# A decoder layer on one core: the last two feed-forward blocks and the per-layer-embedding stage laid out anew

## The reference, cut to what matters

```
hn = rms_norm(h, norm_ffn_w)
gate_pre, val = split(hn @ ffn_w_up)              # 2 x 2816 columns
gate = causal_dwconv(gate_pre, conv_w, conv_b)    # width 3 over the tokens
h = h + (silu(gate) * val) @ ffn_w_down           # 2816 -> 1024
h = h + sigmoid(h @ ple_gate_w) * (p @ ple_w)     # 1024 x 1024, 256 x 1024
return rms_norm(h, final_norm_w)
```

## Time and profile before

| what | us |
|---|---|
| median of three runs (lowest, highest) | 1751.04 (1747.47, 1751.82) |
| the profiled execution, its own time | 1752.36 |
| the profiled execution, its span | 1750.6 |
| PE busy in the span | 1652.4 (94%) |
| DVE busy | 1049.7 (60%) |
| ACT busy | 627.9 (36%) |

### The profile page before, as it was taken

The page is one execution under the profiler, slowest core; times in us unless marked ns, Lnnn a source line. Parts: engine busy times, 40 slices in busy tenths (PEclk is TensorE's granted clock), DMA queues, the critical chain, the costliest instruction groups (busy, mean ns, idle before and its releaser), DMA issues.

```text
span 1750.6 us, 22237 instructions
## 1 busy us (share of the span) xinstructions
PE 1652.4 (94%) x8157; PEld 1334.8 (76%) x8157; DVE 1049.7 (60%) x2090; ACT 627.9 (36%) x1169; POOL 84.9 (5%) x126
## 2 busy tenths in 40 slices
PE   8899999997889999999999999999999999997894
PEld 6688888897656766678888888888888888876673
DVE  6734556555799999854455556556555565546233
ACT  5214344345677777632321221122122122113121
POOL 0101211220000000000000000000000000000002
PEclk9999999998699999999999999999999999998997
DMA  5433232235000000230221121121111112102002
GB/s 192 135 101 115 89 122 87 74 121 160 22 16 13 13 13 1 84 146 1 72 73 37 36 72 36 36 70 38 36 56 52 36 43 64 48 0 96 1 37 84
DMA packets 48874, 110.57 MB, mean 63 GB/s; under 512 B 8864, under 2 KB 17056, under 8 KB 48800
## 3 DMA queue, kind: packets, MB, share of 16 engines
q1 hardware_dynamic: 41376, 85.47, 14.9%
q0 software_dynamic: 7424, 24.12, 4.1%
HBM read 89.65 MB, written 19.92 MB: 63 GB/s over the span
## 4 chain that ended last, share of the span: by engine, by line
PE 81%; DVE 9%; ACT 3%; issue 2%; DMA 1%; POOLq 0%; POOL 0%; DVEq 0%; ACTq 0%
PE ps L1434 27%; PE ps L1088 13%; PE ps L1090 13%; PE ps L1089 13%; PE ps L1234 3%; PE ps L1350 3%; PE ps L1307 2%; PE ps L1313 1%; PE ps L1421 1%; PE ps L1093 1%; PE ps L1352 1%; PE ps L1257 1%; PE ps L1353 1%; DMA out<-ost 1%; DVE mx L1799 1%
## 5 line engine op out<-in xcount | busy, mean ns | idle before, releaser
L1939 DVE TENSOR_TENSOR h<-h,ps 128x512 f32<-128x512 f32 x352 | 236.4, 687 | 158.3 <-PE ps L1090 157.0
L1434 PE MATMUL ps<-htl,wuh 128*128 128x512 f32 x672 | 209.8, 393 | 0.0
L1434 PE MATMUL ps<-hth,wuh 128*128 128x512 f32 x672 | 209.7, 393 | 0.0
L1434 PE MATMUL ps<-hth,wul 128*128 128x512 f32 x672 | 209.7, 393 | 0.0
L1088 PE MATMUL ps<-wh,xth 128*128 128x512 f32 (+1 forms) x448 | 186.7, 417 | 14.6 <-DVE wl L1531 13.0
L1090 PE MATMUL ps<-wh,xtl 128*128 128x512 f32 (+1 forms) x448 | 170.9, 382 | 0.0
L1089 PE MATMUL ps<-wl,xth 128*128 128x512 f32 (+1 forms) x448 | 170.4, 380 | 0.0
L1030 ACT ACTIVATE ffh<-ffa 128x1024 fp32r<-128x1024 f32 x22 | 23.4, 1062 | 381.7 <-DVE ffa L1956 381.7
L1434 PEld LDWEIGHTS ps<-hth,wuh 128*128 128x128 f32 x672 | 126.3, 188 | 29.4
L1434 PEld LDWEIGHTS ps<-hth,wul 128*128 128x128 f32 x672 | 126.2, 188 | 29.2
L1434 PEld LDWEIGHTS ps<-htl,wuh 128*128 128x128 f32 x672 | 126.3, 188 | 28.9
(11 more groups left out here) (269 smaller groups left out, 3206.4 us busy)
## 6 DMA issues: line engine op xcount, KB each, us to landing
wuraw<-in_w_up SPq DMA_DIRECT2D x44, 512.0 KB, 5.5
wraw<-in_w_in SPq DMA_DIRECT2D x48, 256.0 KB, 3.3
proj_d<-stage POOLq DMA_DIRECT2D x48, 256.0 KB, 2.4
wdraw<-in_w_down SPq DMA_DIRECT2D x22, 512.0 KB, 3.5
rin<-proj_d POOLq DMA_DIRECT2D x32, 256.0 KB, 4.0
xraw<-in_xt SPq DMA_DIRECT2D x16, 256.0 KB, 6.1
owraw<-in_w_out SPq DMA_DIRECT2D x8, 512.0 KB, 5.8
h<-in_x SPq DMA_DIRECT2D x1, 4096.0 KB, 16.0
```

The lines of the kernel that those rows point to most:

```text
L1434: mm = nc.tensor.matmul(ps[:, 2 * part + half, :], w_, x_[:, k, half * 512:(half + 1) * 512], start=(k == 0 and i == 0), stop=(k == NK - 1 ...
L1939: nc.vector.tensor_tensor(hh, hh, ps[:, 4 + o_ % 4, :], ALU.add).then_inc(dn_add, 1)
```

## The change

The whole end from block 21 on is written anew.

- **The last two blocks' down products.** `down_part(o_, u)` adds block 20 (u = 0) and block 21 (u = 1) in the same bank, so a unit has six matmuls and one `down_add`. Block 21's value part has nothing woven in. Units 0 to 3 have their first halves right behind it, then come the embedding products of units 0 and 1 into banks 0 and 1 (`part_product`), then the second halves. Block 20 leaves PE's loop and stands in straight code.
- **Weights.** `ple_w` is loaded behind the last feed-forward loads, `pt` after block 20's value part, and both are split by ACT and DVE ahead of their work for block 21 (`part_high`, `part_low`). The gate weights have a place of their own where `hth`/`htl` lay, eight pieces of 128x2x512; their loads are issued together when block 21's value part is done. DVE splits them between the adds by the table `WITH_ADD`.
- **The units** go tile by tile (`t, half = divmod(n, 2)`). Transposes go two tiles ahead, into a ring of three tile buffers (`gth`, `gtl`); the first two stand among the down units (`TURN_ADD`).
- **The norm.** ACT squares each half into a buffer of its own (`sqj`) as soon as it is added; nothing waits for a store there. Each tile is normed while the next one is computed, and the last tile is normed and stored in two halves.

```diff
+        g = Region(nc, START)
+        gwh, gwl, gwraw = [], [], []
+        for i in range(NK):
+            gwh.append(g.put(f"gwh{i}", [P, 2, CH], F32R))
+            gwraw.append(nc.alloc_sbuf_tensor_at(f"gwraw{i}", [P, 2, CH], F32, offset=g.at))
+            gwl.append(g.put(f"gwl{i}", [P, 2, CH], F32R))
+        assert g.at <= OUT_AT
+        NHR = 3
+        gth, gtl = [], []
+        for i, place in enumerate((WU1_AT, WU1_AT + 8 * D, GATE_AT)):
+            g = Region(nc, place)
+            gth.append(g.put(f"gth{i}", [P, NK, P], F32R))
+            gtl.append(g.put(f"gtl{i}", [P, NK, P], F32R))
...
+        def gt_bank(e):
+            return 2 + e % 2 if e < 4 else 4 + e % 4
+
+        LAST_ADDS = OPS * (NF - 2)
+        WITH_ADD = {0: [0], 2: [1], 4: [2], 7: [3], 10: [4], 13: [5], 14: [6], 15: [7]}
+        TURN_ADD = {8: 0, 12: 1}
...
+            sp.dma_start(pwraw[:], ple_w.rearrange("(k p) n -> p k n", p=P)).then_inc(pw_in, 16)
             sp.dma_start(fwb[:], fnw.partition_broadcast(P)).then_inc(wfb_in, 16)
-            for t in range(NT):
+            sp.wait_ge(up_v, NF - 1)
+            sp.dma_start(peraw[:], pt.rearrange("(k p) n -> p k n", p=P)).then_inc(pe_in, 16)
+            sp.wait_ge(up_v, NF)
+            for i in range(NK):
+                half, k = divmod(2 * i, NK)
+                sp.dma_start(gwraw[i][:], ple_gw[k * P:(k + 2) * P, half * CH:(half + 1) * CH].rearrange("(a p) n -> p a n", p=P)) \
+                    .then_inc(gw_in[i], 16)
+            for t in range(NT - 1):
                 sp.wait_ge(fin_done, t + 1)
                 sp.dma_start(out[t * P:(t + 1) * P, :], ost[:, t % 2]).then_inc(out_s[t % 2], 16)
-            for i in range(2):
-                sp.wait_ge(out_s[i], 16 * (NT // 2))
+            t = NT - 1
+            for half in range(2):
+                sp.wait_ge(fin_done, NT + half)
+                cols = slice(half * CH, (half + 1) * CH)
+                sp.dma_start(out[t * P:(t + 1) * P, cols], ost[:, t % 2, cols]).then_inc(out_s[t % 2], 16)
+            sp.wait_ge(out_s[0], 16 * (NT // 2))
+            sp.wait_ge(out_s[1], 16 * (NT // 2 + 1))
...
+            def part_high():
+
+                act.wait_ge(pw_in, PART0 + 16)
+                act.wait_ge(wul_done, 2 * NF)
+                for k in range(NP_):
+                    nc.scalar.activation(pwh[:, k], pwraw[:, k], ACT.Copy).then_inc(gwh_done, 1)
+                act.wait_ge(pe_in, PART0 + 16)
+                for k in range(NP_):
+                    nc.scalar.activation(peh[:, k], peraw[:, k], ACT.Copy).then_inc(gwh_done, 1)
+
             def ffn_act(f, u, q, first, last=False):
                 if first == 0:
                     act.wait_ge(op_done, OPS)
                 if not last:
                     wu_high(f + 1, 1 - u, first == 0)
+                else:
+                    part_high()
...
+            def gw_high(i):
+                act.wait_ge(gw_in[i], GW0 + 16)
+                nc.scalar.activation(gwh[i][:], gwraw[i][:], ACT.Copy).then_inc(gwh_done, 1)
+
+            def gt_high(t):
+                for q in range(2):
+                    e = 2 * t + q
+                    act.wait_ge(gt_full, e + 1)
...
+                    nc.scalar.activation(gth[t % NHR][:, 4 * q:4 * q + 4],
+                                         ps[:, gt_bank(e), :].rearrange("p (k n) -> p k n", k=4), ACT.Copy).then_inc(gt_h, 1)
+
+            def square_out(n):
+                t, half = divmod(n, 2)
+                act.wait_ge(pg_add, n + 1)
+                nc.scalar.activation(sqj[:, n % 2], h[:, t, half * CH:(half + 1) * CH], ACT.Square, scale=1.0 / 32,
+                                     accum_out=fst[:, half, t:t + 1]).then_inc(fsq_done, 1)
+
+            for i in range(4):
+                gw_high(i)
+            gt_high(0)
...
+                t, half = divmod(n, 2)
+                if half and t + 2 < NT:
+                    gt_high(t + 2)
                 act.wait_ge(pg_done, n + 1)
                 if n >= 2:
                     act.wait_ge(pmul_done, n - 1)
-                nc.scalar.activation(sig[:, n % 2], ps[:, n % 2, :], ACT.Sigmoid).then_inc(sig_done, 1)
-                if n > NT:
-                    square_out(n - NT - 1)
-            square_out(NT - 1)
+                nc.scalar.activation(sig[:, n % 2], ps[:, 2 + n % 2, :], ACT.Sigmoid).then_inc(sig_done, 1)
+                square_out(n)
...
-            with pe.Fori(0, NF // 2 - 1) as i:
+            with pe.Fori(0, NF // 2 - 2) as i:
                 ffn_pe(2 * i + 2, 0, None)
                 ffn_pe(2 * i + 3, 1, None)
-            for o_ in range(OPS):
-                down(NF, 1, o_, False)
-
+            ffn_pe(NF - 2, 0, None)
+            pe.wait_ge(gate_ev, NF - 1)
+            up(NF - 1, 1, 0)
+            pe.wait_ge(ffa_done, NF - 1)
+            up(NF - 1, 1, 1)
+
+            def down_part(o_, u):
+
+                t, half = divmod(o_, 2)
+                pe.wait_ge(ffl_done, NF - 1 + u)
+                pe.wait_ge(wdl_done, NF - 1 + u)
+                if u == 0:
+                    pe.wait_ge(dn_add, LAST_ADDS + o_ - 3)
+                _, mm = product(ps[:, 4 + o_ % 4, :], (ffh[:, u, t * P:(t + 1) * P], ffl[:, u, t * P:(t + 1) * P]),
+                                (wdh[:, u, half * CH:(half + 1) * CH], wdl[:, u, half * CH:(half + 1) * CH]), u == 0, u == 1)
+                if u == 1:
+                    mm.then_inc(dn_done, 1)
+
...
+                for k in range(NP_):
+                    product(ps[:, n % 2, :], (peh[:, k, tok], pel[:, k, tok]), (pwh[:, k, cols], pwl[:, k, cols]),
+                            k == 0, k == NP_ - 1)
...
+                    if t < 2:
+                        pe.wait_ge(dn_add, LAST_ADDS + 2 * t + 2)
+                    else:
+                        pe.wait_ge(dn_add, LAST_ADDS + OPS)
+                    if e < 2:
+                        pe.wait_ge(ffa_done, NF)
+                    elif e < 4:
+                        pe.wait_ge(gt_l, e - 1)
+                    elif e >= 8:
...
+            for o_ in range(4):
+                down_part(o_, 0)
+            pe.wait_ge(gate_ev, NF)
+            pe.wait_ge(gwl_done, 2 * NP_)
+            part_product(0)
+            part_product(1)
+            for o_ in range(4):
+                down_part(o_, 1)
+            for o_ in range(4, OPS):
+                if o_ in TURN_ADD:
+                    gt_turn(TURN_ADD[o_])
+                down_part(o_, 0)
+                down_part(o_, 1)
...
+                t, half = divmod(n, 2)
...
+                    part_product(n)
+                if half and t + 2 < NT:
+                    gt_turn(t + 2)
+                if n < 2:
+                    pe.wait_ge(gt_l, 4)
+                else:
                     pe.wait_ge(gt_l, 2 * t + 2)
...
+                hi, lo = gth[t % NHR], gtl[t % NHR]
...
+                    i, a_ = divmod(half * NK + k, 2)
...
+                    _, last = product(ps[:, 2 + n % 2, :], (hi[:, k], lo[:, k]), (gwh[i][:, a_], gwl[i][:, a_]), k == 0, k == NK - 1)
...
+            def part_low():
+                for k in range(NP_):
+                    dve.wait_ge(gwh_done, k + 1)
+                    low(pwl[:, k], pwraw[:, k], pwh[:, k]).then_inc(gwl_done, 1)
+                for k in range(NP_):
+                    dve.wait_ge(gwh_done, NP_ + k + 1)
+                    low(pel[:, k], peraw[:, k], peh[:, k]).then_inc(gwl_done, 1)
+
             def ffn_dve(f, u, q, first, last=False):
                 if not last:
                     wu_low(f + 1, 1 - u)
+                else:
+                    part_low()
 
...
-                if first != 0:
+                if first != 0 and not last:
                     for o_ in range(OPS):
                         down_add(f, o_)
...
+                    e = 2 * t + q
+                    dve.wait_ge(gt_h, e + 1)
...
+            def final_ms(t):
+                dve.wait_ge(fsq_done, FSQ0 + 2 * t + 2)
+                nc.vector.tensor_scalar(fst[:, 2, t:t + 1], fst[:, 0, t:t + 1], fst[:, 1, t:t + 1], EPS, ALU.add, ALU.add) \
+                    .then_inc(fms_done, 1)
...
+            def final_norm(t, cols):
+                dve.wait_ge(frs_done, t + 1)
+                if t >= 2:
+                    dve.wait_ge(out_s[t % 2], 16 * (t // 2))
+                nc.vector.scalar_tensor_tensor(ost[:, t % 2, cols], h[:, t, cols], fst[:, 3, t:t + 1], fwb[:, cols],
...
+                for i in WITH_ADD.get(o_, ()):
+                    gw_low(i)
+                if o_ in TURN_ADD:
+                    gt_low(TURN_ADD[o_])
+                down_add(NF - 1, o_)
+            dve.wait_ge(wfb_in, 32)
+            for n in range(OPS):
+                t, half = divmod(n, 2)
+                if half == 0 and t:
+                    final_norm(t - 1, slice(0, D))
+                if half and t + 2 < NT:
+                    gt_low(t + 2)
+                dve.wait_ge(sig_done, n + 1)
```

(8 more changed lines are left out.)

173 lines of the change are left out of this document (47 added, 126 removed).

## The result

| | median us (lowest, highest) | profiled: own time | span |
|---|---|---|---|
| before | 1751.43 (1747.47, 1752.35) | 1752.36 | 1750.6 |
| after | 1708.3 (1707.47, 1710.54) | 1707.47 | 1705.7 |

What follows compares the result with a forecast made beforehand. PE bound the kernel up to block 21's value part; behind it PE lost about 30 us to waits and low clock, and 24 us followed its last matmul. Saving 30.0 plus 11.0 gave a median of 1710, range 1706 to 1719.

Steps and rivals of the forecast that it cites:

- Value part: Block 21's value part on PE: 48 matmuls at 0.23 us with nothing woven in, 11.0 us, ending at T = 1558.4.
- The joint at no wait: Down units, embedding products and two turns behind block 21's value part: PE never waits, 1 to 3 us spare each place.
- Gate units: PE's gate units after the joint, six turns included: 111.3 us, 6.80 per unit without a turn, bounds 0 to +2.
- a fuller DVE: Gate units: a busier DVE might bring all gate matmuls nearer to 0.233 us, bound 0 to +2 us.
- The tail: From PE's pace end to the span's end: 13.05 us, against 24.1 before, so 11.0 us off.
- The way to the square: From PE's pace end through the last sigmoid, multiply and add to the last square: 2.28 us.
- a square of half the width 0.46 shorter, two half norms 0.10 more, nothing off for the store: From the last square's start to the span's end: 11.13 us before, 10.77 forecast; store bound -1 to +1.
- Rival (b): At the end, two half stores obstruct each other or each pays in full: 2.6 us later, time 1713; chance 0.07.
- The 0.6 us of the estimate: Last store: by the setup-cost rule 3.2 us whole, 2.6 half, so the end 0.6 us earlier; not taken off the forecast.
- Clock: Expected sign: PE's granted clock 1.00 throughout, without idle times over 0.5 us, from 1547 to about 1696.
- rival (c): From T to 1696, pause-free PE is given the lower clock: slower, 1809 if all of it is low; chance 0.03.
- The whole: Span shorter by 41.0 us, 30.0 from PE's end and 11.0 from the tail, to 1709.6; profiled own time 1711.4.

Runs made afterwards that it cites:

- a_ffl_wait: Kernel after, with PE waiting for block 21's `ffl` before its first down unit; median 1716.8 us, ratio 0.9816.
- a_turns_late: Kernel after, with the transposes of tiles 0 and 1 behind the down units instead of among them; median 1714.47 us, ratio 0.981.
- a_ring3: Kernel after, with gate weights loaded three at a time, as through the old ring of three buffers; median 1707.82 us, ratio 0.9779.
- a_port: Kernel after, with idle DVE operations beside POOL's power: two tensor inputs in tiles 1 and 4, one in 2 and 5; 1708.88 us in one run.
- a_woven: Kernel after, with block 20's down product woven into block 21's value part again and 32 adds instead of 16; median 1713.91 us, ratio 0.9803.
- b_square: Kernel before, with ACT's square writing into free PSUM banks and DVE's norm waiting for the store instead; median 1740.46 us, ratio 0.9949.
- b_ kernels: Kernel before with next tile's halves ahead of sigmoid and multiply on ACT and DVE, squares into free PSUM banks, or both; medians 1736.49, 1740.46, 1727.56 us.

## Why the prediction was right, and which step was not

**Value part.** 11.0 us to T = 1558.4; moved by the 4.05 us of the anchor, 1554.35. `ffa` starts at 1554.39. Right.

**The joint at no wait.** First sigmoid 1586.78, forecast near 1591 - 4.05 = 1587. The first weights were taken 3.8 us behind their issue (forecast 3.7) and then 1.3 to 2.1 us apart; the last add ended 3.6 us ahead of the turn. Right. a_ffl_wait and a_turns_late show what two covers were worth (5.5 and 5.2), a_ring3 that issuing all eight loads together was worth nothing.

**Gate units.** 111.3 forecast. From the first sigmoid to the last there are 107.1 us where 105.9 were forecast (6.33, fourteen units of 6.80 and five turns of 0.88). A unit without a turn is 6.85, within the bound of the text (0 to +2):

```profile
1687.01 0.60 ACT L1107 ACTIVATE sig<-ps 128x512 f32<-128x512 f32 x1 [4.05 <-PE ps L1117]
```

(the next, shown above, starts at 1693.86).

The 0.05 in each of fourteen units are 0.7 us. Units 4, 5, 10 and 11 take 0.13 more again (6.98 and 7.84), in every kernel made from after. They are those of tiles 2 and 5, the ones whose transposes lie in the third place of the ring (`GATE_AT`). The prediction's reason, a fuller DVE, does not explain these four: the windows of tiles 2 and 3, equal in work, have DVE busy for the same 5.55 us.

```profile
1607.68:1622.50 14.82, 14.82 (x69) 12.10 (x68) 5.55 (x8) 3.62 (x9) 0.54 (x1) 1.00 0.09 35
1622.50:1637.08 14.58, 14.58 (x69) 12.09 (x68) 5.55 (x8) 3.62 (x9) 0.54 (x1) 1.00 0.10 38
```

No kernel moved the buffers alone, so that the place is the cause is not shown. Together this is the only deviation of PE's path, +1.2.

**The tail**, 13.05 forecast, 12.02 measured. The way to the square is right (2.28 forecast, 2.27 measured). Behind it the step "a square of half the width 0.46 shorter, two half norms 0.10 more, nothing off for the store" is wrong in its mechanism. I read the earlier trace rows as square, power, norm, store, end. The norm and the store were under cover: the end hangs on the end of POOL's power plus 8.16 us. So the terms were the wrong ones, and the one that mattered, the power itself, was carried over at its old length within the 11.13. The tail of before is 14.36 us to the start of that power, 1.52 of power and 8.16 behind it; that of after is 3.32, 0.55 and 8.16. From the square's start to the end it went from 11.10 to 9.75, of which 0.37 is the path to the power and 0.97 the power. Before, DVE was writing the previous tile's norm beside it (1740.73 to 1742.01), now nothing runs beside it; a_port shows this by itself, and before too POOL ended 0.40 us behind DVE's norm. Rival (b), two half stores in each other's way, could not have cost its 2.6 us either: 4.6 us were free behind the landing. The 0.6 us of the estimate from the Trainium skill ("SBUF — State Buffer", The DMA setup-cost knee) could not have shown in the time for the same reason. Its size is another matter: the two half stores took 2.0 to 2.1 us from issue to landing, the whole one 2.6, where the estimate had 2.6 and 3.2, so both differ from it by 0.5 to 0.6, and the difference between them is as it says. That the tail came within 1.0 of the forecast is luck in part: only the way to the square and the half square were sized for the right reason.

**Clock.** 1.00 up to PE's end, 150 us long, so rival (c) did not come; every low stretch between the anchor and PE's end follows, in all kernels, a pause of PE. A pause of 3.7 us was followed by 1.8 us of loss (a_ffl_wait), two of 1.6 and 1.4 by a stretch at 0.50 (a_turns_late), two shorter ones of 0.6 and 0.7 and one of 1.5 by none (a_woven), and of two alike, 2.8 and 2.6 us, the first was followed by a low stretch (before) and the second by none (b_square).

**The whole.** 41.0 forecast from the anchor, 40.8 measured. The sum holds because +1.2 at PE and -1.0 in the tail cancel. Some 2.5 of the 40.8 are the low clock that the profiled execution of before had beyond the b_ kernels; the forecast was counted from the same execution and so has them too. The profiled execution's own time came to 1707.47 where 1711.4 had been forecast, which is the 4.05 us of low clock far ahead of the change. The medians show less of it (1708.3 for 1710), since the profiled execution of before lies above its median and that of after 0.8 below.

## What to carry to other kernels

Ask of each wait of the matrix engine what is queued ahead of its releaser on that releaser's engine: the order of a few lines on ACT and DVE was worth 11.8 us, more than the 10.0 of waits in the list. When one profile is set against another, look for a difference ahead of the place where the edit first acts: 2.5 us of b_square were of that kind. Send no unneeded output into a buffer that a transfer is reading: 10 us. At the end of a kernel compare, over several variants, how far each engine's last operation is from the end: where one stands at a fixed distance, as POOL did here, it and not the data ends the kernel, and taking it off the last step pays (4.4 us). The rows of the engines' sequencers name it.
